# Mixer attention: convolution sums kept in a PSUM bank, and query tiles on another ring of banks

## The reference, cut to what matters

```python
z = h @ w_in                                   # a_val, a_gate (512 each), q (8 heads x 64), k, v (2 x 64)
a = a_val * sigmoid(a_gate)
a = dwconv_centred(a, conv_dw, conv_dw_b)      # 31 taps per channel, 512 channels
a = silu(layernorm(a, conv_ln_g, conv_ln_b))
q, k = rope(rmsnorm(q)), rope(rmsnorm(k))
att = softmax(q k^T / 8) v                     # 8 heads, 2 key/value heads, in 128-query blocks
y = concat(a, att) @ w_out
x = x + rmsnorm(y)
# memory cross attention: 256 memory rows, 4 heads of 256
q = rmsnorm(x) @ w_mem_q;  k, v = rmsnorm(mem) @ w_mem_kv
x = x + rmsnorm(softmax(q k^T / 16) v @ w_mem_o)
# then a gated feed-forward with a 3-tap convolution ("ffn"), and of the second block:
# swiglu f10, pooling mixer, swiglu f20, swiglu f11, latent attention, swiglu f21
```

## Time and profile before

| | us |
|---|---|
| median of 3 runs (lowest, highest) | 2670.73 (2667.22, 2673.47) |
| the profiled execution | 2672.47 |
| its span | 2670.9 |

### The profile page before, as it was taken

The page is one execution under the profiler, slowest core; times in us unless marked ns, Lnnn a source line. Parts: engine busy times, 40 slices in busy tenths (PEclk is TensorE's granted clock), DMA queues, the critical chain, the costliest instruction groups (busy, mean ns, idle before and its releaser), DMA issues.

```text
span 2670.9 us, 28997 instructions
## 1 busy us (share of the span) xinstructions
PE 2583.0 (97%) x11787; PEld 2110.2 (79%) x11787; DVE 1243.9 (47%) x1616; ACT 935.0 (35%) x1376; POOL 628.2 (24%) x471
## 2 busy tenths in 40 slices
PE   8888799999999999999999999999998999999999
PEld 6766677788887888888888888888877787788887
DVE  7896654655625333335333333333335555433322
ACT  4475433444423333224323222322223444322321
POOL 4663301322202222101222101222002322222200
PEclk9998999999999999999999999999998899999999
DMA  4211221232232222322233232332321111232232
GB/s 164 71 40 32 95 63 63 84 98 95 87 98 77 94 95 95 95 91 87 88 102 97 93 95 95 98 100 91 95 89 52 41 42 34 91 105 95 93 95 89
DMA packets 67061, 227.30 MB, mean 85 GB/s; under 512 B 7280, under 2 KB 8816, under 8 KB 66928
## 3 DMA queue, kind: packets, MB, share of 16 engines
q1 hardware_dynamic: 66928, 225.44, 26.5%
HBM read 223.31 MB, written 2.10 MB: 84 GB/s over the span
## 4 chain that ended last, share of the span: by engine, by line
PE 86%; DVE 9%; issue 2%; ACT 2%; POOL 1%; DMA 0%; SPq 0%; DVEq 0%; POOLq 0%; ACTq 0%
PE main L374 19%; PE main L375 19%; PE main L376 19%; PE score L374 6%; PE score L376 6%; PE score L375 6%; PE out L374 3%; PE out L376 3%; PE out L375 3%; DVE cv L581 2%; DVE wl L366 1%; DVE hxl L494 1%; DVE stat L924 1%; DVE pt L959 1%; DVE tmp L1266 1%
## 5 line engine op out<-in xcount | busy, mean ns | idle before, releaser
L366 DVE TENSOR_TENSOR wl<-raw,wh 128x1024 fp32r<-128x1024 f32 (+2 forms) x435 | 563.6, 1298 | 836.7 <-ACT wh L358 836.2
L358 ACT ACTIVATE wh<-raw 128x1024 fp32r<-128x1024 f32 (+2 forms) x435 | 441.1, 1017 | 632.9 <-PE main L376 523.7
L374 PE MATMUL main<-hxh,wh 128*128 128x512 f32 x1264 | 498.6, 394 | 26.9 <-DVE mv_l L1118 14.5
L375 PE MATMUL main<-hxl,wh 128*128 128x512 f32 x1264 | 494.3, 391 | 0.0
L376 PE MATMUL main<-hxh,wl 128*128 128x512 f32 x1264 | 494.0, 391 | 0.0
L374 PE MATMUL main<-hh,wh 128*128 128x512 f32 x880 | 347.7, 395 | 0.7 <-POOL hl L1507 0.5
L376 PE MATMUL main<-hh,wl 128*128 128x512 f32 x880 | 347.5, 395 | 0.0
L375 PE MATMUL main<-hl,wh 128*128 128x512 f32 x880 | 347.5, 395 | 0.0
L374 PEld LDWEIGHTS main<-hxh,wh 128*128 128x128 f32 x1264 | 238.7, 189 | 84.5 <-DVE mv_l L1118 14.9
L376 PEld LDWEIGHTS main<-hxh,wl 128*128 128x128 f32 x1264 | 238.7, 189 | 50.2
L375 PEld LDWEIGHTS main<-hxl,wh 128*128 128x128 f32 x1264 | 238.8, 189 | 48.5
(11 more groups left out here) (376 smaller groups left out, 3502.8 us busy)
## 6 DMA issues: line engine op xcount, KB each, us to landing
raw<-in_wts SPq DMA_DIRECT2D x371, 512.0 KB, 3.6
raw<-in_wts SPq DMA_DIRECT2D x52, 384.0 KB, 3.1
raw<-in_wts SPq DMA_DIRECT2D x12, 256.0 KB, 2.6
x<-in_xT SPq DMA_DIRECT2D x4, 512.0 KB, 8.0
out<-x SPq DMA_DIRECT2D x8, 256.0 KB, 3.9
memx<-in_memT SPq DMA_DIRECT2D x1, 1024.0 KB, 8.6
band<-in_pool SPq DMA_DIRECT2D x1, 768.0 KB, 4.5
rope<-in_rope SPq DMA_DIRECT2D x1, 512.0 KB, 6.3
```

The costliest lines, as they stand in the source:

```text
L358: e.activation(wh[i % NCONV][:, 0:n], raw[i % NRAW][:, 0:n], ACT.Copy).then_inc(*sig.up("weight_high", ("high", i)))
L366: e.tensor_tensor(wl[i % NCONV][:, 0:n], raw[i % NRAW][:, 0:n], f(wh[i % NCONV][:, 0:n]), ALU.subtract) \
L374: e.matmul(o, ah, bh, start=start, stop=False)
L375: e.matmul(o, ah, bl, start=False, stop=False)
```

## The change

From the 37th tap on (place 36), which is turn 0 of attention, VectorE's running sum of a channel tile stays in PSUM bank 7. The first tap of a tile there reads its old sum from cv in SBUF and writes the bank, the next ones read and write the bank, the last one writes cv. Since there is one bank, the taps from place 34 are put in the order of tiles: the 12 of tile 3, then the rest of tile 0, then the rest of tile 1, where tiles 0 and 1 alternated. The numbers of taps and their places in the turns stay.

The memory queries take their banks from a new ring, [3, 4, 7, 0, 1, 2], in place of `wide`, which therefore stands eight takes earlier in all later stages.

```diff
+        query_banks = Ring(banks[3:5] + banks[7:8] + banks[0:3])
...
-        VECTOR_TAPS[34:34] = [(3, j) for j in range(SHARED)]
+        ATTEND_TAP = 36
+        VECTOR_TAPS[34:] = [(3, j) for j in range(SHARED)] + [(c, j) for c in (0, 1) for j in range(20 - 6 * c, CONV_K)]
+        LATE_TAPS = VECTOR_TAPS[ATTEND_TAP:]
+        FIRST_TAP = {c: min(j for d, j in LATE_TAPS if d == c) for c in (3, 0, 1)}
+        LAST_TAP = {c: max(j for d, j in LATE_TAPS if d == c) for c in (3, 0, 1)}
...
+                late = k >= ATTEND_TAP
                 e.wait_ge(*sig.at(("tap", c, j - 1) if j else ("gated", c)))
+                if late and j == FIRST_TAP[c]:
+                    _, old = outb.take(("taps", c))
+                    e.wait_ge(*sig.at(old))
+                old_sum = outb.of(("taps", c))[:, :] if late and j > FIRST_TAP[c] else cv[:, c, :]
+                new_sum = outb.of(("taps", c))[:, :] if late and j < LAST_TAP[c] else cv[:, c, :]
...
-                    made = e.scalar_tensor_tensor(cv[:, c, :], a, w, cv[:, c, :], ALU.mult, ALU.add)
-                made.then_inc(*sig.up("tap_vector", ("tap", c, j)))
+                    made = e.scalar_tensor_tensor(new_sum, a, w, old_sum, ALU.mult, ALU.add)
+                made.then_inc(*sig.up("tap_vector", ("tap", c, j), *([("free", ("taps", c))] if late and j == LAST_TAP[c] else [])))
...
-                _, old = wide.take(("mq", m))
+                _, old = query_banks.take(("mq", m))
...
-                b, old = wide.take(("mq", m))
+                b, old = query_banks.take(("mq", m))
...
-                e.tensor_tensor(s[:, :], wide.of(("mq", m))[:, :], rs[:, :], ALU.mult) \
+                e.tensor_tensor(s[:, :], query_banks.of(("mq", m))[:, :], rs[:, :], ALU.mult) \
```

More of the change, by code:

```diff
@@ L576, in tap_vector @@
                 w, a = col("conv_dw", c * CONV_K + j), apad[:, c, j:j + S]
+                late = k >= ATTEND_TAP
                 e.wait_ge(*sig.at(("tap", c, j - 1) if j else ("gated", c)))
+                if late and j == FIRST_TAP[c]:
[3 more added lines that the diff above has]
+                new_sum = outb.of(("taps", c))[:, :] if late and j < LAST_TAP[c] else cv[:, c, :]
                 if j == 0:
-                    made = e.tensor_scalar(cv[:, c, :], a, w, col("conv_dw_b", c), ALU.mult, ALU.add)
+                    made = e.tensor_scalar(new_sum, a, w, col("conv_dw_b", c), ALU.mult, ALU.add)
                 else:
-                    made = e.scalar_tensor_tensor(cv[:, c, :], a, w, cv[:, c, :], ALU.mult, ALU.add)
-                made.then_inc(*sig.up("tap_vector", ("tap", c, j)))
+                    made = e.scalar_tensor_tensor(new_sum, a, w, old_sum, ALU.mult, ALU.add)
+                made.then_inc(*sig.up("tap_vector", ("tap", c, j), *([("free", ("taps", c))] if late and j == LAST_TAP[c] else [])))
         def tap_scalar(e, k):
@@ L1299, in memory_tensor @@
             for m in range(2):
-                _, old = wide.take(("mq", m))
+                _, old = query_banks.take(("mq", m))
                 e.wait_ge(*sig.at(old))
-            linear_pair(e, U_MQ, wide.of(("mq", 0))[:, :], wide.of(("mq", 1))[:, :], normed("mem"))
+            linear_pair(e, U_MQ, query_banks.of(("mq", 0))[:, :], query_banks.of(("mq", 1))[:, :], normed("mem"))
             for m in range(2, KC):
-                b, old = wide.take(("mq", m))
+                b, old = query_banks.take(("mq", m))
                 e.wait_ge(*sig.at(old))
```

## The result

| | us |
|---|---|
| after: median of 4 runs (lowest, highest) | 2649.51 (2645.13, 2654.95) |
| before, beside it: median of 4 runs | 2672.1 (2667.22, 2675.07) |
| ratio, with its 95% interval | 0.9914 (0.9892 to 0.9935) |
| after, profiled execution (its span) | 2654.95 (2653.2) |
| forecast | 2650.4, range 2643 to 2664 |

Faster, by the size that was forecast. The same kernel, run again with a later group, took 2653.87 (6 runs, ratio 0.9926, 0.9911 to 0.994); the median of all ten runs is 2652.7. The profiled execution is near their upper end, so its own trace shows 17.5 us of gain, where the sum said 20.3. I account for these 17.5 first.

A forecast was written before the change was run, and what follows sets the result against it. VectorE was taken to set attention's pace, slowed by GpSimd's SBUF use; TensorE waited for late query banks. Attention -11.2, queries -10.9, ring shift +1.8 gave -20.3 us: 2650.4 from the 2670.73 median, range 2643 to 2664.

The forecast's parts named there:

- Taps: Attention: 38 convolution taps with their running sum in PSUM take 0.74 us each, where the steady part's mean was 1.218.
- Rival 4: Slower: accumulating in place exposes the PSUM write or collides with neighbouring banks, a tap costs more than now; 2684 us, chance 0.05.
- rival 2: One bank serves reads and writes in turn, a tap takes 1.28 us, attention loses 2.3 us; 2664 us, chance 0.08.
- Steady part: Attention from 151.4 to 219.0: TensorE becomes the bound, its whole idle time of 8.9 us is gained.
- rival 1: Attention: the loop between the engines takes VectorE's place, giving 5 us in place of 11; 2656.6 us, chance 0.16.
- Tail: End of attention, to 231: faster taps gain 1.2 us, where TensorE's slack is 2.2.
- Rival 5: More than forecast: TensorE's clock in head and tail stays up, some 4 us more; 2646 us, chance 0.07.
- Head: Attention's first five turns, 134.0 to 151.4: faster taps gain 1.1 us, where TensorE has 1.77 us of slack.
- Query pair: First two memory query tiles, in banks 3 and 4, start earlier and end 10.2 to 12.1 us earlier; 10.9 taken.
- cap by GpSimd's squares: Memory queries: GpSimd's sum of squares, ending at 338.21, caps the query gain at about 11.5 us.
- Rival 3: Early queries give half, 6 us for 10.9, by TensorE at 1.2 GHz or late squares; 2655 us, chance 0.09.
- Ring shift: Last feed-forward (f11), first gate tile and first down product: two new bank waits of 0.9 us, +1.8 us together.

The follow-up runs named there:

- GpSimd not reading: Kernel of before, with GpSimd's attention additions from its tenth sum on replaced by zero fills of the same SBUF tile: 2647.39 us (one run).
- the short sums: Changed kernel with VectorE's attention convolution sums over 8 columns in place of 512, the other 504 left out: 2654.8 us (one run).
- the order alone: Kernel of before with only the new order of taps, all sums in SBUF, queries on the wide ring: 2664.64 us (one run).
- the earlier low half: Changed kernel with the wide ring realigned, and the second query weight's low half at memory step 3 instead of 4: 2649.62 us, ratio to before 0.9915.
- Realigned: Changed kernel with the wide ring moved on by eight takes at the memory stage: 2647.97 us (ratio to before 0.9907), later 2651.08 (0.9927).

## Why the prediction was right, and where it was not

*Taps: right.* 0.746 us for the predicted 0.74, no spread. Rival 4 and rival 2 fall with the same rows: reading and writing the bank in one instruction costs 10 ns more than L1266, which only reads it (medians 746 and 736). The surcharge for PSUM that the Trainium skill's "Perfetto Trace Analysis" gives (section Optimizing Scalar/DVE Operations) isn't there: in the steady part a tap has a mean of 743 ns in the bank, and of 738 in SBUF with GpSimd not reading.

*Steady part: right.* Predicted 2.26 us per turn, measured 59.10 / 26 = 2.27. TensorE is the bound; rival 1 falls with the short sums.

*Tail: right* at 1.2 us, and VectorE was its bound before: with the order alone its clock rose to 1.00 and it still took 11.84 us. But the 1.2 was taken between 0 and the slack of 2.2, not worked out, so that it fits to a tenth is luck. Rival 5 falls for the tail with the same trace; in the head the clock stayed at 0.90.

*Head: the step failed.* I read "VectorE busy 17.23 of 17.40" as VectorE's pace, and "TensorE has 1.77 us of slack" as slack within the turns. It is one gap at the start, which the moved taps come too late to close; behind it TensorE never waits. The head then goes by the clock. At 0.90 it takes 17.44 and 17.30 us with the taps in SBUF, and 17.00 to 17.20 in six traces with them in the bank: 0.2 to 0.3 us gained for 1.1 forecast. At 0.82 it takes 18.68 with the taps in SBUF (the new ring alone) and 18.47 in the bank (the changed kernel's second trace): again 0.2. One more trace with them in the bank (the earlier low half), at 0.81, has 17.99.

*Query pair: right.* I gave 10.2 for the half-clock case, and 10.3 came, with the end at 334.20 for the predicted 334.3; taking 10.9 between that and the full-clock case was the generous side. The 3.70 us wait is the one worked out (317.5 to 322.2, less the three matmuls). What the sum lacked is behind it, where it had all that follows move up with the pair. The cap by GpSimd's squares bites, which was one of my signs of being wrong. I had their end stay at 338.21; in before's time it is 328.61 + 11.28 = 339.89, and TensorE waits 0.35 us for it. GpSimd's six additions take 11.66 us now, 10.02 before, and beside them VectorE now has three weights' low halves (at 320.36 and from 323.59 to 327.46) where it had one. And TensorE falls to half clock after the square sums, from about 331.5 to 335: eight matmuls at 0.43 us in place of 0.23, 1.6 us. Together the 10.3 became 8.3. Rival 3 said 6 in place of 10.9, by half clock or by the squares; both causes came, at about half of its price.

*Clock falls:* the one at the start of the convolution feed-forward (PEclk 0.96 over 460 to 500) is in each of the eight traces with the query edit and in none of the four without it (1.00). The one after the squares is in seven of the eight, and these are just the seven in which TensorE waits for GpSimd's squares (0.35 to 1.48 us); in the other five of the twelve it doesn't wait and the clock stays. In the kernel with short sums the pair itself stayed at half clock longer, to 317.5, the later fall was absent, and the queries gave 9.1 in place of 8.3. Before each fall TensorE did the 16 one-column matmuls of a sum of squares; the kernel of before has these as well at 489, after a wait of 1.26 us, without a fall. So neither these matmuls nor a wait ahead of them is enough, and what decides was not found.

*Ring shift: right.* Two waits, named in place and releaser, 0.79 us each where I had 0.9; 2.1 us in the difference between the traces, for 1.8 forecast. Realigned, both go, and nothing else waits in their place.

*The sum.* Head 0.8 too much, queries 2.6 with what follows, the next stage's clock 1.6, against 3.4 us in my favour, by the clock (1.6 behind attention, 1.8 late); the small rest is in the table. The total came out within 3 us, and the median of the first four runs within 1, by parts that are partly luck of the clock: the layer norm takes 41.9 us at 0.84 or 40.35 at 0.87, with the same instructions, in kernels with and without the change.

## What to carry to other kernels

Moving one operand of a VectorE instruction from SBUF to PSUM can be enough: it no longer takes turns with GpSimd's reads (1218 ns became 743), and the instruction stays on its engine. In the head a busy share of 17.23 of 17.40 did not name the bound, since the other engine's idle time was one single gap; look at its waits one by one first. A ring that loses takes shifts all stages behind it, and advancing it by the same number of takes puts them back.

## What was not expected of the hardware

- VectorE takes 0.746 us for 128x512 with the sum read from and written to one PSUM bank, for 0.743 with everything in SBUF while GpSimd only fills (medians of 32 and 39 taps). A tile's first sum, which has one tensor as input, takes 0.53 us from SBUF to SBUF undisturbed, 1.50 ahead of attention in the changed kernel, and 0.80 into the bank.
- A sum over 8 columns takes 218 ns, one over 512 takes 743: on a straight line between the two, an estimate, 1.04 ns for a column and 0.21 us that stay however short it is.
- Executions of one kernel differ in where the clock is granted: the latent stage took 319.5 and 317.8 us in two traces of the changed kernel, and between 310.8 and 320.2 over all kernels here, with TensorE idle for the same 17.8 us where I looked (310.8 - 293.1, 313.7 - 295.9, 317.8 - 300.0, 319.5 - 301.7). One trace's late difference of some 2 to 6 us says nothing about a change that isn't there.
